# Value products for two query heads at a time, and equal runs of keys in the score products, in a hybrid decoder layer

## What is computed

```python
def query_block(c):                       # 8 blocks of 128 queries
    s_s = einsum('bqhgd,bhqsd->bhgqs', qc, ks) * scale + bias_s   # keys 0 .. t
    o_s = einsum('bhgqs,bhqsd->bqhgd', masked_softmax(s_s), vs)
    s_w = einsum('bqhgd,bkhd->bhgqk', qc, kw) * scale + bias_w    # last 512 keys
    o_w = einsum('bhgqk,bkhd->bqhgd', masked_softmax(s_w), vw)
o = g[..., 0:1] * o_cmp + g[..., 1:2] * o_sel + g[..., 2:3] * o_win
x = x + concatenate([y_ssm, o]) @ w_out
```

## Time and profile before

| what | value |
|---|---|
| median of 3 runs | 1066.81 us (1064.61 to 1067.37) |
| the profiled execution's own time | 1067.54 us |
| TensorE busy, of the span | 992.8 us, 93% |
| its span, first to last instruction | 1065.6 us |
| mean granted TensorE clock | 0.968 |
| stage_attend in the trace | about 355 to 579 us |
| output projection and router | about 579 to 711 us |
| experts | about 711 us to the end |

### The profile page before, as it was taken

The page is one execution under the profiler, slowest core; times in us unless marked ns, Lnnn a source line. Parts: engine busy times, 40 slices in busy tenths (PEclk is TensorE's granted clock), DMA queues, the critical chain, the costliest instruction groups (busy, mean ns, idle before and its releaser), DMA issues. The chain is left out here.

```text
span 1065.6 us, 13459 instructions
## 1 busy us (share of the span) xinstructions
PE 992.8 (93%) x5091; PEld 578.9 (54%) x5091; DVE 488.1 (46%) x1221; ACT 276.5 (26%) x621; POOL 149.9 (14%) x146
## 2 busy tenths in 40 slices
PE   6999999999999899999999999996999888899991
PEld 4436787666555566666766455563454333444440
DVE  3495490396555377666663224273731111211115
ACT  3201111302123576565653101110001000100124
POOL 4000000130211221111011000011221101212130
PEclk9999999999999899999999999986999899999996
DMA  9400240224200650000000234455889999999965
GB/s 257 126 27 4 79 79 0 28 18 119 61 1 1 147 177 2 1 2 1 1 2 1 98 138 147 185 201 217 294 301 344 360 409 396 393 391 397 385 214 216
DMA packets 61744, 165.79 MB, mean 156 GB/s; under 512 B 32747, under 2 KB 34859, under 8 KB 49319
## 3 DMA queue, kind: packets, MB, share of 16 engines
q1 hardware_dynamic: 53296, 145.99, 38.5%
q0 software_dynamic: 8096, 18.42, 6.8%
q10 hardware_dynamic: 288, 0.53, 0.1%
HBM read 147.41 MB, written 25.24 MB: 162 GB/s over the span
## 5 line engine op out<-in xcount | busy, mean ns | idle before, releaser
L2007 PE MATMUL banks<-shared,wout 128*64 128x512 f32 (+1 forms) x416 | 149.4, 626 | 14.0 <-issue 12.3
L1615 PE MATMUL banks<-wout,shared 128*128 128x512 f32 x256 | 112.7, 594 | 0.5 <-PEq L1275 0.5
L2007 PEld LDWEIGHTS banks<-shared,wout 128*64 128x64 f32 (+1 forms) x416 | 56.6, 170 | 88.5 <-issue 88.0
L1323 ACT ACTIVATE shared<-shared,low 128x640 f32<-128x640 f32 (+7 forms) x128 | 92.9, 729 | 3.0 <-DVE low L1410 2.5
L2055 DVE SCALAR_TENSOR_TENSOR mix_bt<-mix_bt,slot_coef,banks 128x256 f32<-128x256 f32 x24 | 11.5, 480 | 170.5 <-ACT mix_bt L2035 170.4
L384 PE MATMUL banks<-x,wout 128*128 128x512 f32 x192 | 84.6, 595 | 0.8 <-DVE x L425 0.8
L1373 PE MATMUL banks<-consts,shared 128*128 128x128 f32 x528 | 79.2, 286 | 2.1 <-ACT shared L1323 1.3
L1373 PEld LDWEIGHTS banks<-consts,shared 128*128 128x128 f32 x528 | 56.9, 142 | 41.8 <-issue 36.9
L1615 PEld LDWEIGHTS banks<-wout,shared 128*128 128x128 f32 x256 | 47.6, 190 | 55.2 <-issue 55.2
L2029 PE MATMUL banks<-shared,hidt 128*64 128x512 f32 (+1 forms) x208 | 72.5, 596 | 1.9 <-DVE wout L2070 1.3
L1355 PE MATMUL banks<-shared 64*128 64x512 f32 (+3 forms) x384 | 72.0, 492 | 1.9 <-PEq L994 1.3
(11 more groups left out here) (364 smaller groups left out, 1283.7 us busy)
## 6 DMA issues: line engine op xcount, KB each, us to landing
shared<-in_exp_w_down SPq DMA_DIRECT2D x26, 1024.0 KB, 18.1
shared<-in_exp_w_gate SPq DMA_DIRECT2D x26, 1024.0 KB, 16.6
shared<-in_exp_w_up SPq DMA_DIRECT2D x26, 1024.0 KB, 21.6
x<-in_exp_w_gate SPq DMA_DIRECT2D x6, 1024.0 KB, 16.5
x<-in_exp_w_up SPq DMA_DIRECT2D x6, 1024.0 KB, 24.3
x<-in_exp_w_down SPq DMA_DIRECT2D x6, 1024.0 KB, 25.7
wout<-in_w_in SPq DMA_DIRECT2D x16, 256.0 KB, 5.1
wout<-in_w_in SPq DMA_DIRECT2D x2, 2048.0 KB, 8.1
```

The lines of the kernel that those rows point to most:

```text
L1323: nc.scalar.activation(prob[:, u % 2, at:at + n], prob[:, u % 2, at:at + n], ACT.Exp, bias=low[:, u % 2, v, j:j + 1], scale=-1.0, accum_ou ...
L1615: ins = nc.tensor.matmul(psum[n % 4], src[:, i * P:i * P + P], m["wout"][:, k, half * 512:half * 512 + 512], start=k == 0, stop=k == KD - 1)
L2007: ins = nc.tensor.matmul(psum[2 + p][rows].rearrange("p (a f) -> p a f", a=2), xt[:, p, k, rows], wgu[b][:, :, k], start=k == 0, stop=k == ...
```

## The change

Value products take two query heads at a time: units 2k and 2k+1 are a pair. Their transposed probabilities lie in one buffer with two halves, and one matmul now streams 256 columns, 128 of each unit. The pair's key blocks are split in two halves: the first half is multiplied in pass 2k+2, the second in pass 2k+3, and both halves of the last pair after the loop. The mix follows one pass later. The second of the two pair buffers is the upper half of `x1`, so x is loaded back in two parts: tiles 0 to 3 at the start as before, tiles 4 to 7 when all value products are done. In a unit of one branch the score products take two equal runs of keys.

```diff
-    pt = [m["pt0"], m["pt1"]]
+    pt = m["pt_pairs"]
...
-            sp.dma_start(m["x1"][:], d["x"][0].rearrange("(i p) n -> p i n", p=P)).then_inc(m["x_in"], 16)
+            x_back = d["x"][0].rearrange("(i p) n -> p i n", p=P)
+            sp.dma_start(m["x1"][:, 0:4], x_back[:, 0:4]).then_inc(m["x_in"], 16)
+            sp.wait_ge(m["x_in"], 16)
+            sp.wait_ge(pv_done, len(units) // 2)
+            sp.dma_start(m["x1"][:, 4:8], x_back[:, 4:8]).then_inc(m["x_in"], 16)
...
-            if u >= 2:
-                eng.wait_ge(pv_done, u - 1)
+            if u >= 4:
+                eng.wait_ge(pv_done, u // 2 - 1)
             w = len(what) * P
-            copy(pt[u % 2][:, n0 * P:n0 * P + w], bank[:, 0:w]).then_inc(t_out[r % 2], 1)
+            copy(pt[u // 2 % 2][:, u % 2, n0 * P:n0 * P + w], bank[:, 0:w]).then_inc(t_out[r % 2], 1)
...
-                    cut = b[-1] * P + P - 512
-                    spans = [(0, b[0] * P, cut, brs[0]), (1, cut, cut + 512, brs[0])]
+                    end = b[-1] * P + P
+                    cut = (b[0] * P + end) // 2
+                    spans = [(0, b[0] * P, cut, brs[0]), (1, cut, end, brs[0])]
                 for n, (j, k0, k1, br) in enumerate(spans):
-                    c0 = 512 - (k1 - k0) if len(brs) == 1 else 0
+                    c0 = 512 - (k1 - k0) if len(brs) == 1 and j == 0 else 0
...
-            def outputs(u):
+            def outputs(u, part):
                 c, i, brs = units[u]
-                for r in of_unit[u][-2:]:
-                    pe.wait_ge(t_out[r % 2], r // 2 + 1)
-                if i == 0 and c:
-                    for br in brs:
-                        pe.wait_ge(o_out, 2 * c - 1 + br)
+                if part == 0:
+                    for r in of_unit[u][-2:] + of_unit[u + 1][-2:]:
+                        pe.wait_ge(t_out[r % 2], r // 2 + 1)
+                    if i == 0 and c:
+                        for br in brs:
+                            pe.wait_ge(o_out, 2 * c - 1 + br)
...
                     b = blocks(c, br)
-                    for n, kb in enumerate(b):
+                    cut = (len(b) + 1 - j) // 2
+                    for n, kb in list(enumerate(b))[cut * part:len(b) if part else cut]:
                         for v in range(KV):
                             half, at = slice(v * HD, v * HD + HD), where[v, j, n]
-                            ins = nc.tensor.matmul(psum[6 + br][half, i * P:i * P + P], vals[:, kb, half],
-                                                   pt[u % 2][:, at * P:at * P + P], start=n == 0, stop=n == len(b) - 1)
-                ins.then_inc(pv_done, 1)
+                            ins = nc.tensor.matmul(psum[6 + br][half, i * P:i * P + 2 * P].rearrange("p (h q) -> p h q", h=2),
+                                                   vals[:, kb, half], pt[u // 2 % 2][:, :, at * P:at * P + P],
+                                                   start=n == 0, stop=n == len(b) - 1)
+                if part:
+                    ins.then_inc(pv_done, 1)
...
-                if u >= 1:
-                    outputs(u - 1)
+                if u >= 2:
+                    outputs(u - 2 - u % 2, u % 2)
                 transposes(u, rounds_of[u][2:])
-            outputs(len(units) - 1)
+            for part in range(2):
+                outputs(len(units) - 2, part)
...
-                    got = m["banks"][:, (v + 1) * 1024 - n:(v + 1) * 1024]
+                    got = m["banks"][:, v * 1024 + 512 - n // 2:v * 1024 + 512 + n // 2]
...
-                if u and mixed[u - 1]:
-                    dve.wait_ge(pv_done, u)
-                    for c, br in mixed[u - 1]:
+                if u > 1 and mixed[u - 2]:
+                    dve.wait_ge(pv_done, u // 2)
+                    for c, br in mixed[u - 2]:
...
-        dve.wait_ge(m["x_in"], 16)
         dve.wait_ge(m["r_in"], 16 * 8)
...
         def residual(i, half):
             n = 2 * i + half
+            if half == 0 and i in (0, 4):
+                dve.wait_ge(m["x_in"], 32 if i else 16)
...
+            ends = shared[:, 8 * T:24 * T].rearrange("p (h n) -> p h n", h=8)[:, 0:8:7]
+            m["pt_pairs"] = [ends, m["x1"][:].rearrange("p (b t) n -> p b (t n)", t=2)[:, 2:4]]
```

## The result

| | before | changed |
|---|---|---|
| median of 9 runs | 1066.04 us (1064.61 to 1067.81) | 1068.39 us (1066.03 to 1071.02) |
| ratio, with its 95% interval | | 1.0025 (1.0014 to 1.0036) |
| the profiled execution's own time, its span | 1067.54, 1065.6 us | 1066.41, 1064.5 us |
| stage_attend, first score product to first output projection | 224.57 us | 227.04 us |

The change costs 0.25%, 2.35 us between the medians, close to the 2.4 forecast, and inside the 0.3% that was called no change. The interval leaves out 1, so the loss is real, and its upper end (0.36%) lies a little above those 0.3%.

A forecast was written before the change was run, and what follows sets the result against it. It took TensorE's streamed columns, plus about 7 us of waits, to bound the attention stage. Terms -0.7 - 0.15 - 0.2 + 3.4 - 0.4 + 0.5 = +2.4 us gave a median of 1069.2 us, range 1065.2 to 1072.0.

The forecast's parts named there:

- The steps: Value products: 264 steps of 256 columns replace 528 of 128, -0.7 us; one value phase fewer, -0.15 us.
- The rival of a fixed cost that the rows hide: Value products: wide steps save more than streaming shows; 24 ns a step would give 1063.6 us or less; chance 0.08.
- The scores: Score products with equal key runs: 5 to 10 ns saved on each affected unit, -0.2 us in all.
- Work that lands under waits: Value products moved between passes of stage_attend: time taken from in front of waits is not gained, together +3.4 us.
- the remainders: Passes 5 and 19 and small remainders in the wide early passes: +0.4 us, between 0 and 0.7.
- The barrier: End of stage_attend: the sync queue issues a 2 MB load before the barrier, +0.5 us, bounds 0.2 and 1.0.
- The sum: All terms for the whole kernel: +2.4 us, a median of 1069.2 us, counted as no change.
- Busy near 58 us: Sign that the forecast is right: value products in 528 records, busy near 58 us.
- Window passes that together are shorter than 2 x 3.92: Sign that the forecast is wrong: two window passes in stage_attend together shorter than 2 x 3.92 us.
- The longer low clock: Rival, first units: 1.2 GHz lasts one more stretch, some 0.9 us not hidden, 1070.1 us; chance 0.30.
- The pair that doesn't stream as one: Rival, value products: two runs of 128 columns cost a start each, 2.6 us per 10 ns a step; chance 0.07.
- Waits swallowing less: Rival, passes 13 to 41: VectorE's copies come earlier, so 2.3 us are not lost, 1066.9 us; chance 0.10.

The follow-up runs named there:

- experiment 1: The kernel before with only the equal runs of keys in the scores of one-branch units; ratio 1.0000, stage 224.60 us.
- experiment 10: The changed kernel run and traced once more, with nothing altered; 1067.3 us in one run, stage 227.33 us.
- experiment 4: The changed kernel with the smaller half of a one-branch pair's key blocks multiplied first; ratio 1.0013, stage 226.54 us.
- experiment 7: The changed kernel with VectorE's copy of round 1 between the next unit's two bias instructions in chosen passes; ratio 0.9992, stage 223.26 us.
- experiment 3: The changed kernel with the second load of x moved behind the barrier; ratio 1.0014, stage 227.31 us.
- experiment 9: The changed kernel with early VectorE copy and late x load, units 0 to 3 multiplied singly and pairs from unit 4; ratio 0.9985, stage 222.44 us.
- experiment 6: The kernel before with VectorE's copy of round 1 between the next unit's two bias instructions in chosen passes; ratio 0.9973, stage 221.97 us.
- experiment 5: The changed kernel with both halves of a pair multiplied in the even pass, none in the odd; ratio 1.0197, stage 246.90 us.

## Why the prediction was right

**The steps.** Forecast 0.215 to 0.216 us for a step of 256 columns, measured 0.2158, against 2 x 0.1092 for two of 128; fixed part of a phase 0.15. That is 2.6 ns a step, and the 0.7 + 0.15 us saved stand. The rival of a fixed cost that the rows hide (0.08) falls with it. The rule of the Trainium skill that was weighed ("TensorEngine Tiling (Array Packing)", section "Instruction Overhead"), read as a cost added to each step, would make one step of 256 columns about 25 ns cheaper than two of 128, near 0.19 us by an estimate from its figure; the trace, at 0.2158, disagrees with that reading.

**The scores.** Forecast -0.2, measured -0.08 (experiment 1).

**Work that lands under waits.** The list of passes held. Forecast and measured change of a pass: pass 13 0 and 0.00; pass 41 -0.12 and -0.11; 33 about -0.2 and -0.17; 40 and 32 0 and 0.00; 23, 31 and 39 0 and 0.00. Of the remainders, pass 19 lost 0.19 under its copies; pass 5, named beside it, lost nothing and kept its whole gain of 0.44. Past the first four passes the time in front of copies and in transposes grew by 2.21 us, where the terms of these passes add up to 3.4 - 1.05 = 2.35. For passes 0 to 3 the forecast's remaining terms about cancel; measured were -0.03 us in the first trace and +0.26 in experiment 10.

The stage grew by 2.47; without steps (-0.85), scores (-0.08) and barrier (+0.59) that leaves 2.81 for waits and clock together, where the forecast had 3.4 - 0.4 = 3.0. Experiments 4 and 7 show that it is these waits. Work put under them is free (4). With the copy earlier the changed kernel got 4.1 us shorter past the first four passes, where the kernel before got 2.7: the loss of the change there, without the barrier, fell from 1.9 to 0.5 us. The time in front of copies that it had gained shrank from 2.2 to 0.2, and 0.5 of held score products came up.

**The barrier.** Forecast +0.5, from 0.39 for the issue and 0.1 for a drain; measured +0.59 (experiment 3). The issue took 0.37. No run shows the 0.1 as such: 0.09 us pass from the last value product to the issue, and from the end of the issue to the first projection 0.60, which is 0.13 more than the 0.47 of before.

**The sum.** +2.4 against +2.47 in the stage and +2.35 between the medians. That all three lie within 0.1 us is in part luck. The trace behind the 2.47 is the cheap case of passes 0 to 3 (15.82 us); in experiment 10, with the longer low clock, the same kernel's stage grew by 2.76. The medians carry the scatter of the rest of the kernel, and how many of the nine runs had the longer low clock isn't known.

**The signs.** Two of those written down were wrong in themselves. "Busy near 58 us": the value products are busy 67.9 us, 1.3 less than before; 264 steps of 0.2158 alone are 57.0, and the fixed part of 47 phases and the tail of each row come on top. "Window passes that together are shorter than 2 x 3.92" was to show the forecast wrong, and passes 20 and 21 take 7.80; but its own terms, 1.45 + 1.02 where 2 x 1.25 stood, give 7.81. And pass 41 takes the 5.75 of the sum, not the 5.65 of the sign.

**The rivals.** The longer low clock, given 0.30, is real, and the sum has no term for it: it came in six of eight traces of kernels without the phase of pass 1, and in one of the two of the changed kernel itself. Its price was overstated: 0.2 to 0.9 us above the 15.9 of passes 0 to 3 (16.11 to 16.76), and in the other two traces the level fell later and cost nothing, so a mean near 0.4 where 0.9 was written. Experiment 9 ties it to the value phase of pass 1. The page "TensorE: Matmul & The Clock Gate" of the Trainium skill, section "What's actually happening", says that activity is what releases the throttle; the stretches of the earlier trace rows and of experiments 3 and 9 agree with it (the level rose behind 3.30, 3.40 and 3.30 us busy of 3.40). The pair that doesn't stream as one didn't occur. Waits swallowing less didn't either: the scores' end didn't move (experiment 1).

What the chances didn't say is that the best use of the same reading was elsewhere: the waits of which the earlier trace rows show four, 0.28 to 0.78 us each, are worth 2.6 us to the kernel before (experiment 6), more than the about 1 us of steps, phase and scores that the change could have given.

## What to carry to other kernels

Halving the instruction count saved 0.7 us here, since 0.213 of a step's 0.2158 us were streamed columns. So take two phases of unequal length, divide out the price of a step and of a phase, and see what is left before rebuilding a schedule around wide matmuls. When work is moved between passes, price it by what the receiving and the giving pass wait for; work taken from in front of a wait is not gained, and work added there is free as far as the wait reaches. The wait itself is often the cheaper thing to change: here one VectorE copy, put between two long instructions and not behind both, beat the kernel before (0.9973). Its stage, 221.97 us, is also shorter than that of every version of the change tried (222.44 and up), though the interval of its ratio overlaps with that of the best of them (0.9985). It has a price of its own: the later bias then holds score products.

## What was not expected

- An idle TensorE in the first units moved the clock in two ways: in six traces the low level lasted 13.7 us instead of 10.2, in two it came later and lasted 6.8. Both occur with the same kernel (experiment 10 and the first trace of the changed one). What decides between them is open.
- The low level came back in the middle of the busy attention stage: behind 4 us in which TensorE was busy 2.20, 1.2 GHz was granted for 6.8 us (experiment 5), and again for 3.4 us a little later; two passes took 9.2 to 9.3 us instead of 5.9.
- What lies behind the stage varied by 3.7 us between traces (482.5 to 486.2) with the same work for TensorE in it. The first 131.5 us of it agree, so the scatter lies in the last router products and the experts. Why was not tried.
